# Expert stage of a two-block transformer kernel with 112 in place of 128 token slots per expert

## What is computed

```python
def moe_swiglu(h, w_router, wg, wu, wd):
    xt = h.reshape(-1, D)
    logits = (xt @ w_router).astype(jnp.float32)
    top_v, top_i = lax.top_k(logits, TOP_K)
    gates = jax.nn.softmax(top_v, axis=-1)
    gate = jnp.sum(jax.nn.one_hot(top_i, N_EXPERTS, dtype=jnp.float32) * gates[..., None], axis=1)
    y = jnp.zeros_like(xt)
    for e in range(N_EXPERTS):
        y = y + gate[:, e:e + 1].astype(xt.dtype) * swiglu(xt, wg[e], wu[e], wd[e])
    return y.reshape(B, S, D)
```

## Time and profile before

| | us |
|---|---|
| time, median of 3 runs | 2694.66 |
| lowest and highest run | 2694.05, 2695.15 |
| span of the profiled execution | 2690.4 |
| TensorE busy in it | 2616.0 |
| VectorE busy in it | 2068.6 |
| ScalarE busy in it | 1536.7 |

### The profile page before, as it was taken

One profiled execution on the slowest core, in us unless ns is written; L12 is line 12 of the kernel. 1 busy time (PEld: TensorE's weight loads), 2 busy tenths in 40 slices (PEclk: granted clock), 3 DMA queues, 4 the chain that ended last, 5 costly groups with the idle time before them and its releaser, 6 DMA issues.

```text
span 2690.4 us, 48898 instructions
## 1 busy us (share of the span) xinstructions
PE 2616.0 (97%) x19438; PEld 2463.6 (92%) x19438; DVE 2068.6 (77%) x2783; ACT 1536.7 (57%) x2198; POOL 189.3 (7%) x257
## 2 busy tenths in 40 slices
PE   8999999999999999999999999998999999998999
PEld 8899988999999999999999899986999999887999
DVE  4677766988988898988889778667788787576654
ACT  4643455777777777777777633545433433445432
POOL 2001020000000000000000111012111010021000
PEclk9999998999999999999999999999999999999999
DMA  7277534998989898989899678431587577431452
GB/s 287 112 298 302 203 127 147 331 354 311 359 312 349 320 354 313 351 324 348 321 349 348 262 275 314 172 134 48 212 311 287 218 302 275 165 118 48 165 188 87
DMA packets 76822, 679.22 MB, mean 252 GB/s; under 512 B 8641, under 2 KB 8769, under 8 KB 27969
## 3 DMA queue, kind: packets, MB, share of 16 engines
q1 hardware_dynamic: 55440, 599.10, 60.0%
q0 software_dynamic: 21168, 77.08, 7.1%
HBM read 675.10 MB, written 1.05 MB: 251 GB/s over the span
## 4 chain that ended last, share of the span: by engine, by line
PE 85%; DVE 7%; ACT 4%; issue 2%; DMA 1%; POOL 0%; DVEq 0%; SPq 0%; ACTq 0%; POOLq 0%
PE ps L1697 23%; PE ps L1698 23%; PE ps L1699 23%; PE ps L2222 11%; PE ps L2187 1%; DVE w_parts L1462 1%; PE ps L2231 1%; PE ps L2197 1%; ACT w_parts L927 1%; DMA ring<-wstream 1%; DVE a_lo L1469 1%; DVE xT L1538 1%; ACT sq L609 1%; DVE pT L1070 1%; PE ps L1991 0%
## 5 line engine op out<-in xcount | busy, mean ns | idle before, releaser
L1697 PE MATMUL ps<-a_hi,w_parts 128*128 128x256 f32 x2544 | 727.9, 286 | 13.8 <-DVE a_lo L1089 6.3
L1698 PE MATMUL ps<-a_lo,w_parts 128*128 128x256 f32 x2544 | 720.7, 283 | 0.0
L1699 PE MATMUL ps<-a_hi,w_parts 128*128 128x256 f32 x2544 | 720.5, 283 | 0.0
L1462 DVE TENSOR_TENSOR w_parts<-ring,w_parts 128x1024 fp32r<-128x1024 f32 x448 | 547.9, 1223 | 70.2 <-ACT w_parts L927 68.4
L1697 PE MATMUL ps<-w_parts 128*128 128x256 f32 x1792 | 528.5, 295 | 0.1
L1697 PEld LDWEIGHTS ps<-a_hi,w_parts 128*128 128x128 f32 x2544 | 488.5, 192 | 24.8 <-issue 16.8
L1698 PE MATMUL ps<-w_parts 128*128 128x256 f32 x1792 | 506.1, 282 | 0.0
L1699 PE MATMUL ps<-w_parts 128*128 128x256 f32 x1792 | 505.7, 282 | 0.0
L1698 PEld LDWEIGHTS ps<-a_lo,w_parts 128*128 128x128 f32 x2544 | 488.6, 192 | 1.5 <-issue 1.4
L1699 PEld LDWEIGHTS ps<-a_hi,w_parts 128*128 128x128 f32 x2544 | 488.9, 192 | 0.0
L927 ACT ACTIVATE w_parts<-ring 128x1024 fp32r<-128x1024 f32 x448 | 472.3, 1055 | 2.0 <-DMA ring<-wstream 2.0
(11 more groups left out here) (250 smaller groups left out, 4099.6 us busy)
## 6 DMA issues: line engine op xcount, KB each, us to landing
ring<-wstream SPq DMA_DIRECT2D x378, 1536.0 KB, 8.0
proj<-astream POOLq DMA_DIRECT2D x144, 512.0 KB, 6.1
cst<-consts SPq DMA_DIRECT2D x1, 1700.0 KB, 15.4
vtok<-crow POOLq DMA_DIRECT2D x3, 512.0 KB, 3.9
xT<-x_in SPq DMA_DIRECT2D x1, 1024.0 KB, 5.2
out<-xT SPq DMA_DIRECT2D x1, 768.0 KB, 3.3
proj<-wpool SPq DMA_DIRECT2D x1, 512.0 KB, 15.5
out<-xT SPq DMA_DIRECT2D x1, 256.0 KB, 3.3
```

What stands on the lines that cost most here:

```text
L1462: nc.vector.tensor_tensor(up_lo[:, n % 2, at], ring[:, s, at], up_hi[:, n % 2, at], ALU.subtract).then_inc(xup_lo, 1)
L1697: mm(o, stationary[0], moving[0], start=start, stop=False, skip_group_check=True)
L1698: mm(o, stationary[0], moving[1], start=False, stop=False, skip_group_check=True)
L1699: return mm(o, stationary[1], moving[0], start=False, stop=stop, skip_group_check=True)
```

## The change

`CAP` goes from 128 to 112. The slot buffers keep their size and layout; every instruction that reads or writes slots is cut to 112 of them, on partitions where slots lie there, and in columns where they lie along the free axis. The limit at which the wide form is taken falls with it, from more than 128 to more than 112 tokens at one expert. The constant row `slots` is 112 wide. The diff, cut to its main lines; ScalarE's edits come first, then VectorE's, then TensorE's:

```diff
-CAP = 128
+CAP = 112
...
-                nc.scalar.activation(he_hi[:, n_e % 2, 4 * half:4 * half + 4, :],
-                                     ps[:, bank, :].rearrange("p (k c) -> p k c", k=4), ACT.Copy)\
+                nc.scalar.activation(he_hi[:, n_e % 2, 4 * half:4 * half + 4, 0:CAP],
+                                     ps[:, bank, 0:4 * CAP].rearrange("p (k c) -> p k c", k=4), ACT.Copy)\
...
-                        nc.scalar.activation(sg[:, n % 2, 0:P], ps[:, 4 + n % 2, 0:P], ACT.Silu)\
+                        nc.scalar.activation(sg[0:CAP, n % 2, 0:P], ps[0:CAP, 4 + n % 2, 0:P], ACT.Silu)\
...
-                            nc.scalar.activation(ye[:, c * 512:(c + 1) * 512],
-                                                 ps[:, 2 * ((n_e - 1) % 2) + c, :], ACT.Copy).then_inc(ye_ready, 1)
+                            nc.scalar.activation(ye[0:CAP, c * 512:(c + 1) * 512],
+                                                 ps[0:CAP, 2 * ((n_e - 1) % 2) + c, :], ACT.Copy).then_inc(ye_ready, 1)
...
-                nc.vector.tensor_tensor(he_lo[:, n_e % 2, at, :],
+                nc.vector.tensor_tensor(he_lo[:, n_e % 2, at, 0:CAP],
...
-                    nc.vector.tensor_scalar(dst[:, e, tt, :], C("slots"), rt[:, 1, tt, e:e + 1],
+                    nc.vector.tensor_scalar(dst[:, e, tt, 0:CAP], C("slots"), rt[:, 1, tt, e:e + 1],
...
-                        nc.vector.tensor_tensor(hid[:, n % 2, 0:P], sg[:, n % 2, 0:P], ps[:, 4 + n % 2, P:2 * P],
+                        nc.vector.tensor_tensor(hid[0:CAP, n % 2, 0:P], sg[0:CAP, n % 2, 0:P], ps[0:CAP, 4 + n % 2, P:2 * P],
...
-                        moving = (place[:, n_e, tt, :] if isinstance(r, int) else
+                        moving = (place[:, n_e, tt, 0:CAP] if isinstance(r, int) else
...
-                    nc.tensor.transpose(ps[:, 6, 0:CAP], hid[:, n % 2, 0:P], C("ident")).then_inc(xturn_ready, 1)
+                    nc.tensor.transpose(ps[:, 6, 0:CAP], hid[0:CAP, n % 2, 0:P], C("ident")[0:CAP, 0:CAP]).then_inc(xturn_ready, 1)
...
-                        ins = mm3(ps[:, 4 + b, 0:T], (he_hi[:, n_e % 2, k, :], he_lo[:, n_e % 2, k, :]),
+                        ins = mm3(ps[0:CAP, 4 + b, 0:T], (he_hi[:, n_e % 2, k, 0:CAP], he_lo[:, n_e % 2, k, 0:CAP]),
...
-                            ins = mm(ps[:, bank + half, :], h[:, b, 0:CAP], w[:, b, half * D // 2:(half + 1) * D // 2],
+                            ins = mm(ps[0:CAP, bank + half, :], h[:, b, 0:CAP], w[:, b, half * D // 2:(half + 1) * D // 2],
...
-                        ins = mm(ps[:, bank + d % 4 // 2, (d % 2) * T:(d % 2 + 1) * T], ye[:, d * P:(d + 1) * P],
+                        ins = mm(ps[:, bank + d % 4 // 2, (d % 2) * T:(d % 2 + 1) * T], ye[0:CAP, d * P:(d + 1) * P],
...
-                                ins = nc.tensor.transpose(ps[:, 7, j * P:(j + 1) * P],
-                                                          gplace[:, 2 * i + j // 2, j % 2, :], C("ident"))
+                                ins = nc.tensor.transpose(ps[0:CAP, 7, j * P:(j + 1) * P],
+                                                          gplace[:, 2 * i + j // 2, j % 2, 0:CAP], C("ident"))
```

More of the change, by code:

```diff
@@ L990, in expert @@
                             act.wait_ge(gp_ready, i + 1)
-                            nc.scalar.activation(scatter[:, 2 * i:2 * i + 2, :],
-                                                 ps[:, 7, :].rearrange("p (e t) -> p e t", e=2),
+                            nc.scalar.activation(scatter[0:CAP, 2 * i:2 * i + 2, :],
+                                                 ps[0:CAP, 7, :].rearrange("p (e t) -> p e t", e=2),
                                                  ACT.Copy).then_inc(gp_copied, 1)
@@ L1000, in moe_fast @@
                 for c in range(2):
-                    nc.scalar.activation(ye[:, c * 512:(c + 1) * 512], ps[:, 2 * ((NE - 1) % 2) + c, :], ACT.Copy)\
+                    nc.scalar.activation(ye[0:CAP, c * 512:(c + 1) * 512], ps[0:CAP, 2 * ((NE - 1) % 2) + c, :], ACT.Copy)\
                         .then_inc(ye_ready, 1)
@@ L1514, in tokens @@
                 at = slice(4 * half, 4 * half + 4)
-                nc.vector.tensor_tensor(he_lo[:, n_e % 2, at, :],
-                                        ps[:, bank, :].rearrange("p (k c) -> p k c", k=4),
-                                        he_hi[:, n_e % 2, at, :], ALU.subtract).then_inc(xg_lo, 1)
+                nc.vector.tensor_tensor(he_lo[:, n_e % 2, at, 0:CAP],
+                                        ps[:, bank, 0:4 * CAP].rearrange("p (k c) -> p k c", k=4),
+                                        he_hi[:, n_e % 2, at, 0:CAP], ALU.subtract).then_inc(xg_lo, 1)
             def moe_fast():
@@ L1624, in router @@
                 for tt in range(TT):
-                    nc.vector.tensor_scalar(place[:, 0, tt, :], C("slots"), rt[:, 1, tt, 0:1],
+                    nc.vector.tensor_scalar(place[:, 0, tt, 0:CAP], C("slots"), rt[:, 1, tt, 0:1],
                                             rt[:, 0, tt, 0:1], ALU.is_equal, ALU.mult)\
@@ L2184, in gather @@
                     for tt in range(TT):
-                        moving = (place[:, n_e, tt, :] if isinstance(r, int) else
-                                  place[:, bass.ds(r + n_e, 1), tt, :].rearrange("p a c -> p (a c)"))
+                        moving = (place[:, n_e, tt, 0:CAP] if isinstance(r, int) else
+                                  place[:, bass.ds(r + n_e, 1), tt, 0:CAP].rearrange("p a c -> p (a c)"))
                         ins = mm(ps[:, bank, (k % 4) * CAP:(k % 4 + 1) * CAP],
@@ L2228, in scatter_half @@
                     for d in range(4 * half, 4 * half + 4):
-                        moving = (scatter[:, n_e, :] if isinstance(r, int) else
-                                  scatter[:, bass.ds(r + n_e, 1), :].rearrange("p a t -> p (a t)"))
-                        ins = mm(ps[:, bank + d % 4 // 2, (d % 2) * T:(d % 2 + 1) * T], ye[:, d * P:(d + 1) * P],
+                        moving = (scatter[0:CAP, n_e, :] if isinstance(r, int) else
+                                  scatter[0:CAP, bass.ds(r + n_e, 1), :].rearrange("p a t -> p (a t)"))
+                        ins = mm(ps[:, bank + d % 4 // 2, (d % 2) * T:(d % 2 + 1) * T], ye[0:CAP, d * P:(d + 1) * P],
                                  moving, start=d % 2 == 0, stop=True, skip_group_check=True)
```

## The result

| | before | after |
|---|---|---|
| median, us (runs) | 2694.68 (4) | 2675.81 (4) |
| lowest and highest run | 2694.05, 2695.15 | 2672.50, 2680.15 |
| span of the profiled execution | 2690.4 | 2673.5 |

After stands to before as 0.993 (95% interval 0.9917 to 0.9944): the change takes 18.9 us, where 5.3 were forecast, and the time lies 0.2 us under the low end of the range. The two profiled executions differ by 16.9 us. Every run of before and after whose span is listed stands 1.6 to 1.8 us above it (after: 2675.17 over 2673.5, 2672.50 over 2670.7), so the profiled execution of before took about 2692.1 us. The 4.3 us that I put around the program were 1.7, and the rest was scatter. That scatter is larger than the four runs of before show: further runs of the same kernel, beside the experiments, lie between 2689.50 and 2696.98 us.

The account below looks back on a forecast made before the run. TensorE was taken to bound the 134 plain chunk steps and VectorE the about 90 longer ones. Terms of 1.5 + 1.5 + 0.9 + 0.5 + 0.7 = 5.1 us, with a little overhead 5.3, gave 2689.4 us; range 2676 to 2693.5 us.

Parts of the forecast that it names:

- the step on the up and down products: Expert chunks' 5376 up and 1344 down products: 112 stationary columns for 128 were to gain 0 us.
- Loads are thus below the pace of 0.120 already: Up products: weight loads, near 0.112 us, were taken as shorter than the 0.120 us matmul pace, so not limiting.
- The second argument: Matmul before the transpose keeps its 0.12 us although the load beside it is short, 141 ns against 190.
- The bound between the two cases: Up and down products: overhead paid per loaded column would gain 1.7 and about 2.5 ns per product, 7.5 us.
- the long steps: About 90 of 224 chunk steps, longer than 4.37 us, where VectorE sets the time; hid_lo's 17 ns gains 1.5 us.
- Rival A: Loads pace the up products: gaps towards 0.109 us, TensorE's chunk 4.10, VectorE's 4.21 us then limits; 2670 us; chance 0.10.
- The rest of the sum: Transposes 1.5 us, hid_lo 1.5, token parts 0.9, placement rows 0.5, cold gathers with their token parts 0.7: 5.1 us.
- the other limit that I named: At transpose L2197, the next up product's load might stay the limit; lower bound 0 us, 1.5 us forecast.
- The cold gathers: First 32 gathers, at granted clock 0.50 with the load hidden: about 18 gain 27 ns each, 0.5 us.
- B: Fixed costs swallow the gain in transposes and copies; only the first gathers gain; about 2694 us; chance 0.15.
- C: Switching the array between 112 and 128 columns costs 0.09 us, two switches per chunk; 2725 us; chance 0.04.
- D: Narrow path not taken, wide plain fp32 products run instead; chunk 10.4 us, time 4030 us less the gathers; chance 0.01.

Follow-up runs that it names:

- The series: Kernel before plus series of 48 matmuls each on TensorE behind its last product, with varied stationary and moving columns; 2849.92, 2876.98 and 2847.64 us, one run each.
- the third experiment: Kernel before with only the up and down products loading 112 stationary columns, transposes, copies and gathers kept at 128; 2681.25 us, 0.9948 of before.
- with fewer bytes: The change with two thirds of each tile transferred in the expert stage, down weights left out; 2671.18 us, 0.9921 of before.
- the first experiments: First four kernels: the change with up products (2688.97 us) or down products (2679.84) at 128 again; before with only both loads cut (2681.25); 96 slots (2674.02).

## Why the prediction was wrong

**What failed** is the step on the up and down products: "I take 0 for these products." Their stationary sizes alone are worth 12.9 us. Undone one by one in the change, and each time against the before beside it, the up products cost 13.7 us and the down products 4.6. Together that is more than the 12.9, and the traces show two ways in which the parts act on each other: down products of 128 raise the up gap from 115.9 to 117.0 ns, and up products of 128 take back what the transpose had gained. The argument behind the 0 was the earlier trace rows: 384 moving columns stand 0.013 us above their time at 2.4 GHz, 256 moving ones as well, so I read a constant that has nothing to do with the load. The series show two different things of one size. At 384 columns it is the moving side's own cost, which no smaller load changes (174.0 and 173.4 ns). At 256 it is that cost, 7 to 11 ns, and the rest comes with a load of 111.6 ns that is nearly as long as the matmul beside it. One row at another size could not tell the two apart.

That the load's time is what counts is argued from this closeness. The stationary columns are also the partitions that a product writes, 112 or 128, and no run here parts the two.

**"Loads are thus below the pace of 0.120 already"** was true and did not settle it. A limit that lies 7% below the pace was taken as none. The listed load fell to 175 ns, near the 177 of the forecast, and not "with nothing following from it". The second argument, the short load beside the matmul in front of the transpose, looked at one gap; the change moved 22 of them.

**The bound between the two cases** was too small for the up products: 1.7 ns each where 3.6 were seen. For the down products it had 2.5 ns, and the last four gaps of a group show 2.2. With these sizes its 7.5 us would have been 134 x (24 x 3.6 + 6 x 2.2) ns = 13.3, and with the 5.3 of the sum the forecast would have been 18.6 us. That 18.9 were measured is partly luck: the first gap of a down group gained nothing, 21 or 22 gaps of a chunk gained and not 24, the cold gathers gave nothing, and against these stands a gain in the long steps, for which neither the bound nor the sum had a term of TensorE's.

**Rival A** named the side that mattered, the load of the up products, and had the chance 0.10. Of its numbers, the pace was to fall to 0.109 us and fell to 0.116, where it stays with 96 and 88 columns; the chunk was to reach 4.10 and VectorE's 4.21 us to take over, and TensorE still sets the step, at 4.28. Its 2670 us are 6 below the measured time, my forecast 14 above.

**The rest of the sum** came out near, in part by luck. The two stationary sizes alone leave 6.0 us to the rest of the change, each against its own before, where the sum had 5.1 for transposes, copies and gathers; no run takes these one by one. The transpose gained 11 ns (0.229 to 0.218 us from L2197 to the second L1698, by the averages), which is the 1.5 us forecast, and the other limit that I named, the load behind it, is real. hid_lo, hid_hi and the token part came out at 268, 264 and 619 ns, the placement rows 9 ns shorter and not 17. The long steps are 0.33 us per expert shorter than with the stationary sizes alone, some 2 us in all, which is the copies' part. What is left is an up gap that is lower in the change than with the same sizes in the third experiment, 115.9 for 116.5 ns, and nothing in the sum stood for that. The long steps also hold a part of TensorE's: 0.76 us per expert in the change and 0.38 where the up products are undone, so about half, in steps that I had given to VectorE alone.

**The cold gathers** were to gain 0.5 us and gained nothing: at the granted clock of 0.50 the load is not hidden. Loads, and with them the matmuls, start 213 ns apart in that stretch before and after, although the moving side shrank; in the stage it is 111 to 112 ns. The load keeps pace with the array's clock, and I had charged it at the full one. (The 32 listed instructions are 16 matmuls, two halves of eight; a plain fp32 matmul counts twice.)

**B, C and D** did not happen. No gap of 0.2 us appears at L2197 apart from the transpose's own, so 112 stationary columns cost no switch; with 120, 96 and 88 it is the same. The narrow form was taken throughout.

**What stays open** is why a stream keeps to levels, why 118 columns run faster than 116, what decides between 113.3 and 117.7 ns, and what the down products gained by. The runs of the change scatter over 7.7 us (2672.5 to 2680.2). Single late tiles of about 1 us each would fit, and with fewer bytes the runs lie within 3.5 us; but the kernel before scatters over 7.1 us in thirteen runs beside the first experiments, with few such waits in its trace, so this was not shown.

## What to carry to other kernels

When a matmul's moving time and its weight load are within some 5% of each other, the shorter one may not be free: cutting 16 of 128 stationary columns took 3% off the pace of 256-column fp32r products, and cutting 32 or 40 took no more. At 264 moving columns, 8% above the load, the same cut gave nothing. To say which side bounds a pace, vary one side alone in a short series at the end of the kernel; two rows of the trace at different sizes can agree by chance. And judge a pace by the mean over the stage, since one chunk's 0.118 us for 0.119 hid a gain of some 13 us.

## What the runs showed of the hardware

- An fp32r matmul in a stream costs 113.3 to 120.0 ns with 256 moving columns, about 174 with 384 and 227 with 512, and for these two no less with a smaller stationary side; a stream bound by weight loads costs 111.6 ns with 128 columns and 98.3 with 112. The Trainium skill, page "TensorE: Matmul & The Clock Gate", section "LDWEIGHTS (loading the stationary operand)", gives columns over 1.2, by which I estimate 107 and 93 ns; the trace agrees with the slope and stands 5 ns above.
- That load slows with TensorE's clock: at a granted 0.50 (1.2 GHz) loads of 128 columns come 0.213 us apart, at 1.00 (2.4 GHz) 0.112.
- One stream has more than one steady pace: with 112 columns 113.3 or 117.7 ns for the same instructions and operands.
- Stationary operands of 72 to 127 columns start as one of 128 does, 112 to 121 ns after the last with 256 moving columns; those of 16 in the earlier trace rows did not.
